# Residual kept by token tiles: norms on rows, 512-column out and down products, gates as broadcast rows

## The chip, the cores and the metric

The kernel runs on one core of one Trainium2 chip. The core has five engines that run side by side and meet by semaphores: TensorE (PE; its weight loads are listed apart as PEld), VectorE (DVE), ScalarE (ACT), GpSimd (POOL) and SyncE (SP, here used for loads). The metric is the device time of one execution in microseconds; lower is better. All data is fp32.

## The reference, cut to what matters

A two-layer backbone runs over 640 tokens of width 1024: 128 context tokens and 512 latent tokens, each group with its own modulation vectors. One layer:

```
shift1, scale1, gate1, shift2, scale2, gate2 = split(silu(cond) @ w_mod + b_mod)      # 6 x 1024
h = rmsnorm(x, g_mix) * (1 + scale1) + shift1
z = h @ w_in                                  # 2720 columns, feed four token mixers
branches = four mixer outputs (256 each) @ w_branch                                   # to 1024
mixed = sum(sigmoid(h @ w_gate + b_gate) * branches) @ w_out
x = x + gate1 * mixed
h2 = rmsnorm(x, g_ffn) * (1 + scale2) + shift2
u = h2 @ w_up + b_up; conv = depthwise width 3 over tokens; a, gg = split(conv)       # 2 x 2816
x = x + gate2 * ((silu(gg) * a) @ w_down)
```

A last rmsnorm with g_final gives the outputs. The mixers (retention, window attention, differential attention, latent attention) are the same before and after the change.

## The kernel before, in words

Every large product is made of three products of rounded parts: each fp32 operand is split in a high part (fp32r) and a low part (the rest), and high x high, low x high and high x low are summed in PSUM. For weights ACT rounds the high part (`round_unit`, L1436) and POOL subtracts the low part (L767); for activations ACT and DVE do it. Weights come in units of up to 1 MB in the order of `weight_units`, through three raw buffers and two pairs of high/low slots. Every engine runs one list of instructions in the order in which the program issues them; nothing is reordered between them, and all order is written out by hand.

The residual x is held channel by channel: 8 tiles k of 128 channels on the partitions, 640 tokens along the free dimension. What hangs on that:

- The in product (`in_product`, L914) holds 128 tokens of h as the stationary operand and moves 512 columns of the weights. Its output z has tokens on partitions.
- The gate, out, up and down products (`product3`, L819) hold 128x128 of the weights and move tokens, 320 or 322 at a time (two halves), in the out product's tiles 5 to 7 and the first two up tiles 256 and 384.
- The out product's result is added to x by `add_to_x` (L2230), one operation per token piece, with the gate as a per-partition scalar. `take_out` follows with the squares (`add_square`, L2222 and L2224). The sum over channels needs PE: `part_sums` (L880) multiplies the squares by ones, ACT takes the root, DVE the reciprocal and a diagonal, and `spread_part` (L887) brings it back to all partitions. `part_norm` then scales, modulates and splits x into h_hi and h_lo, in two parts of 256 and 384 tokens, so that the first up tiles (`first_up`) can start on the first part.
- The down product (`down_tiles`, `down_part`) runs in three groups of 8, 8 and 6 activation tiles. In the last group the last k of the first tiles is put off until its activation is ready. `take_down` adds the result to x.
- At a layer's start `mod_pair` (L841) computes the first eight modulation columns in four pairs: per pair 16 matmuls of 256 columns, each on a quarter of the array, the four k of a quarter round summed afterwards by `fold_pair` (L850). In both layers they lie in or ahead of the first in product.
- At the start of the kernel 40 transposes (L791) bring x into this layout, at the end 40 transposes (L1404) bring it back; `token_sums`, `spread_rstd` and L1397 do the sums in between.
- x itself is stored in DRAM while the mixers use its room as the sum `acc`, and is loaded back on ACT's queue during the last gates.

The prediction's steps touch `in_product`, the out loop, `first_up`, `down_tiles`, `mod_pair` on PE, the norm functions on ACT and DVE, and SP's list of loads.

Of the kernel before, what the change touches and what calls it, by code (L numbers as in the profile page):

```python
# [60 lines left out]
ACT_SLOTS = 12  # L61
# [3 lines left out]
def mlp_order():  # L65

    items = []
    for g, (j0, nj) in enumerate(UP_GROUPS):
        first = j0 + (AHEAD if g else 0)
        items += [("up", j) for j in range(first, j0 + nj)]  # L70
        if g + 1 < len(UP_GROUPS):
            n0 = UP_GROUPS[g + 1][0]
            items += [("up", j) for j in range(n0, n0 + AHEAD)]
        items += [("down", (g, mp)) for mp in range(4)]
    return items
# [52 lines left out]
def weight_units():  # L128

    mod = iter(MOD_ORDER)  # L130
    win = lambda g: [("in", (g, half), True) for half in range(2)]
    mods = lambda n: [("mod", next(mod), False) for _ in range(n)]
    gate = lambda n, mp: [("gate", (n, mp), True)]
    first, second = win(0)
    units = mods(2) + [first] + mods(4) + [second] + mods(2) + win(1) + gate(0, 0) + gate(0, 1) + win(2)
    units += gate(0, 2) + mods(1) + gate(0, 3) + mods(3) + [("in", (3, 0), True)] + mods(2) + [("in", (3, 1), True)] + win(4) + win(5)
    units += gate(1, 0) + gate(1, 1) + mods(2) + gate(1, 2) + mods(1) + gate(1, 3) + mods(1) + gate(2, 0)
    units += [("uq", 0, False)] + gate(2, 1) + [("ukv", 0, False)] + mods(2) + gate(2, 2) + mods(1) + gate(2, 3)
# [6 lines left out]
OUT_TILES = [(m, None) for m in range(5)] + [(m, 0) for m in range(5, KD)] + [(m, 1) for m in range(5, KD)]  # L145
OUT_BANK = {(5, 0): 4, (6, 0): 5, (7, 0): 2, (5, 1): 3, (6, 1): 1, (7, 1): 5}
OUT_BEHIND = {(7, 0): (3, None), (5, 1): (3, None), (6, 1): (4, None), (7, 1): (6, 0)}
CUT = 2 * P
PARTS = (slice(0, CUT), slice(CUT, TOK))
PART_TILES = (range(0, 2), range(2, T))  # L150
WHOLE = ((0, 0, CTX), (1, CTX, TOK))
PIECES = (((0, 0, CTX), (1, CTX, CUT)), ((1, CUT, TOK),))


UNITS = weight_units()
N_UNITS = len(UNITS)
N_SPLIT = sum(split for _, _, split in UNITS)
RAW = 3
WS = 2
SPLIT_KEYS = [(kind, i) for kind, i, split in UNITS if split]  # L160
LOW_BY_VECTOR = [("in", (0, 0)), ("in", (0, 1))]
LOW_BY_POOL = [key for key in SPLIT_KEYS if key not in LOW_BY_VECTOR]
# [18 lines left out]
def part_slot(li, s):  # L181

    return WS if SLOT[s] == WS else (SLOT[s] + li * FLIP) % WS

# [94 lines left out]
def build(nc, a, outs):  # L279
# [3 lines left out]
    with ctx:  # L283
# [12 lines left out]
        x = at("x", [P, KD, TOK])  # L296
# [6 lines left out]
        vcol = at("vcol", [P, 317])  # L303
        cond = at("cond", [P, 16])
# [76 lines left out]
        acc = x  # L381
        x_saved = nc.dram_tensor("x_saved", [P, KD, TOK], F32).ap()

        sq = at("sq", [P, TOK], offset=BASE + 82272)
        ss = at("ss", [P, TOK], offset=BASE + 84832)
        t1 = at("t1", [P, 2, TOK], offset=NT + 5120)
        sq_b = at("sq_b", [P, 3, TOK - CUT], offset=NT + 10240)
        diag = at("diag", [P, T, P], offset=NT + 15360)

        a_hi = at("a_hi", [P, ACT_SLOTS, PADDED], F32R, offset=BASE)  # L390
        a_lo = at("a_lo", [P, ACT_SLOTS, PADDED], F32R, offset=BASE + 30816)
        FB = BASE + 61632
# [5 lines left out]
        x_tm = at("x_tm", [P, T, D], offset=BASE)  # L398
        y_tm = at("y_tm", [P, T, D], offset=BASE + 20480)
        g_fin = at("g_fin", [P, D], offset=BASE + 40960)  # L400
# [19 lines left out]
        def x_ready(m, part):  # L420

            return OUT_TILES.index((m, part)) + 1

# [3 lines left out]
        def pair_col(li, p):  # L427

            return 5 * BANK if p else 3 * BANK if li else 7 * BANK + P
# [16 lines left out]

        raw_loaded = [Signal(f"raw_loaded{i}", loaded_count(max(range(i, N_UNITS, RAW)))) for i in range(RAW)]
        hi_done, lo_done = Signal("w_high_ready", N_SPLIT), Signal("w_low_ready", len(LOW_BY_POOL))
# [1907 lines left out]
```

## Time and profile before

| | us |
|---|---|
| median of 3 runs | 2431.77 |
| lowest, highest | 2429.27, 2432.41 |
| profiled execution | 2432.2 |
| its span, first to last instruction | 2430.4 |

The page says that PE is busy for 2363.8 us, PEld for 2144.0, DVE for 1244.4, ACT for 879.1 and POOL for 731.8. The mean granted clock of PE is 0.993 of full speed. A matmul's busy time includes its way through the array, so consecutive matmuls overlap in the records: what a stream of them costs is read from the distance of their starts, not from their mean duration. An fp32 matmul that is not rounded leaves two records, a transpose one. "Idle before <- X" names what the engine waited for.

### The profile page before, as it was taken

How to read it: one execution, taken by the hardware profiler on the slowest of the kernel's cores; microseconds unless marked ns; L12 is line 12 of the kernel's file. 1: busy time of each engine (PE TensorE's matmuls, PEld its weight loads, DVE VectorE, ACT ScalarE, POOL GpSimd, SP SyncE). 2: the span in 40 equal slices, each digit the busy share in tenths (PEclk: the TensorE clock that was granted, in tenths of full speed). 3: DMA queues.
4: the chain of work that ended last, by engine and by line, in shares of the span. 5: the costliest groups of instructions: out<-in, count | busy, mean ns of one | idle time of the engine just before them, and what ended most of it. 6: DMA issues, size and time to landing. Idle time of an engine off the chain costs nothing.

```text
span 2430.4 us, 38405 instructions
## 1 busy us (share of the span) xinstructions
PE 2363.8 (97%) x16085; PEld 2144.0 (88%) x16085; DVE 1244.4 (51%) x2251; ACT 879.1 (36%) x1642; POOL 731.8 (30%) x500
## 2 busy tenths in 40 slices
PE   7999999999999999999999999999999999999998
PEld 5887787788999999999978878887889999999997
DVE  5426247534347762753763362673433677447356
ACT  4335245534324431332243352555343243223231
POOL 0321221101342453444312203210113435435432
PEclk9999999999999999999999999999999999999999
DMA  8413221222331322222271132312232312222211
GB/s 291 143 55 122 66 91 59 74 70 87 109 92 53 104 70 70 87 70 61 79 269 55 53 124 72 102 46 71 87 104 85 98 53 70 87 70 70 87 53 53
DMA packets 234154, 216.48 MB, mean 89 GB/s; under 512 B 8310, under 2 KB 217598, under 8 KB 233726
## 3 DMA queue, kind: packets, MB, share of 16 engines
q1 hardware_dynamic: 225911, 193.77, 25.0%
q10 hardware_dynamic: 8071, 20.25, 2.4%
q8 instruction: 128, 2.10, 0.3%
q14 instruction: 44, 0.36, 0.0%
HBM read 204.92 MB, written 9.08 MB: 88 GB/s over the span
## 4 chain that ended last, share of the span: by engine, by line
PE 88%; DVE 5%; ACT 3%; POOL 2%; issue 1%; DMA 0%; ACTq 0%; DVEq 0%
PE ps L819 58%; PE ps L914 11%; PE ps L968 4%; PE ps L1021 2%; POOL w_lo L767 2%; PE ps L1038 2%; PE ps L1000 2%; PE ps L1010 2%; PE ps L829 1%; ACT w_hi L1436 1%; DVE h_lo L1891 1%; PE ps L989 1%; DVE t L1883 1%; PE ps L859 1%; PE ps L1214 1%
## 5 line engine op out<-in xcount | busy, mean ns | idle before, releaser
L767 POOL TENSOR_TENSOR w_lo<-raw,w_hi 128x512 fp32r<-128x512 f32 x488 | 718.9, 1503 | 1664.3 <-ACT w_hi L1436 1048.8
L819 PE MATMUL ps<-h_hi,w_hi 128*128 128x320 f32 (+2 forms) x2368 | 618.4, 314 | 4.0 <-POOL w_lo L767 4.0
L819 PE MATMUL ps<-h_lo,w_hi 128*128 128x320 f32 (+2 forms) x2368 | 608.8, 310 | 0.0
L819 PE MATMUL ps<-h_hi,w_lo 128*128 128x320 f32 (+2 forms) x2368 | 608.7, 310 | 0.0
L819 PEld LDWEIGHTS ps<-h_hi,w_hi 128*128 128x128 f32 x2368 | 415.1, 189 | 8.8 <-issue 4.3
L819 PEld LDWEIGHTS ps<-h_lo,w_hi 128*128 128x128 f32 x2368 | 415.0, 189 | 0.8
L819 PEld LDWEIGHTS ps<-h_hi,w_lo 128*128 128x128 f32 x2368 | 415.0, 188 | 0.0
L1436 ACT ACTIVATE w_hi<-raw 128x2048 fp32r<-128x2048 f32 (+2 forms) x110 | 203.7, 1851 | 307.3 <-PE ps L819 219.0
L1986 DVE TENSOR_REDUCE stat<-ps 128x1 f32<-128x640 f32 (+3 forms) x160 | 107.9, 674 | 174.7 <-PE ps L1010 113.9
L914 PE MATMUL ps<-w_hi,h_hi 128*128 128x512 f32 (+1 forms) x480 | 182.8, 381 | 6.8 <-DVE h_lo L1891 3.8
L914 PE MATMUL ps<-w_hi,h_lo 128*128 128x512 f32 (+1 forms) x480 | 180.1, 375 | 0.0
L914 PE MATMUL ps<-w_lo,h_hi 128*128 128x512 f32 (+1 forms) x480 | 180.1, 375 | 0.0
L2230 DVE SCALAR_TENSOR_TENSOR x<-ps,mod,x 128x128 f32<-128x128 f32 (+4 forms) x192 | 72.9, 434 | 192.7 <-PE ps L819 192.0
L819 PE MATMUL ps<-a_hi,w_hi 128*128 128x322 f32 x704 | 162.6, 312 | 2.2 <-DVE a_lo L2297 1.4
L2282 DVE TENSOR_SCALAR conv<-u_pad,vcol 128x642 f32<-128x642 f32 x88 | 91.9, 1044 | 141.4 <-ACT u_pad L1788 139.8
L819 PE MATMUL ps<-a_hi,w_lo 128*128 128x322 f32 x704 | 161.7, 311 | 0.0
L819 PE MATMUL ps<-a_lo,w_hi 128*128 128x322 f32 x704 | 161.4, 310 | 0.0
L1796 ACT ACTIVATE usig<-conv 128x642 f32<-128x642 f32 x44 | 32.7, 744 | 261.3 <-DVE conv L2286 261.3
L968 PE MATMUL ps<-o_t,w_br 128*128 128x320 f32 x384 | 125.3, 450 | 0.0
L819 PEld LDWEIGHTS ps<-a_hi,w_hi 128*128 128x128 f32 x704 | 118.9, 190 | 3.3 <-DVE a_lo L2297 1.9
L2284 DVE SCALAR_TENSOR_TENSOR conv<-u_pad,vcol,conv 128x642 f32<-128x642 f32 x88 | 118.4, 1345 | 3.1
L819 PEld LDWEIGHTS ps<-a_lo,w_hi 128*128 128x128 f32 x704 | 118.8, 189 | 0.0
(299 smaller groups left out, 3330.0 us busy)
## 6 DMA issues: line engine op xcount, KB each, us to landing
raw<-in_w_mod SPq DMA_DIRECT2D x48, 1024.0 KB, 5.1
raw<-in_w_up SPq DMA_DIRECT2D x88, 512.0 KB, 4.6
raw<-in_w_gate SPq DMA_DIRECT2D x32, 1024.0 KB, 5.7
raw<-in_w_in SPq DMA_DIRECT2D x20, 1024.0 KB, 5.5
raw<-in_w_down SPq DMA_DIRECT2D x16, 1024.0 KB, 5.2
w_br<-in_w_branch ACTq DMA_DIRECT2D x8, 1024.0 KB, 5.0
raw<-in_w_out SPq DMA_DIRECT2D x8, 1024.0 KB, 5.2
raw<-in_w_down SPq DMA_DIRECT2D x8, 768.0 KB, 4.8
```

Source lines behind the costliest of these rows:

```text
L767: ins = nc.gpsimd.tensor_tensor(w_lo[part_slot(li, s)][:, c0:c1], raw[u % RAW][:, c0:c1], w_hi[part_slot(li, s)][:, c0:c1].bitcast(F32), A ...
L819: ins = mm(out, w_at(w_hl[wi]), at_(x_hl[xi]), start=first and q == 0, stop=final and q == 2)
L914: last = mm(bank(b, 0, n), (h_hi, h_lo)[xi][:, k, t * P:(t + 1) * P], w_hl[wi][:, k4, :], start=k == 0 and q == 0, stop=k == KD - 1 and q ...
L968: last = mm(bank(FILL_BANK[("branch", q)], 0, HALF), w_br[:, k, m * P:(m + 1) * P], o_t[n % 2][:, k, half * HALF:(half + 1) * HALF], start ...
L1000: last = mm(bank(2 * m2, col, col + n), query(br, t, h, m2), keys(br, h, m2, k0, n), start=True, stop=True)
L1010: last = mm(bank(2 * (m % 2), col, col + n), query(br, t, h, 0), keys(br, h, 0, k0, n), start=True, stop=True)
L1021: last = mm(ps[64 * odd:64 * odd + 64, 6 * BANK + 64 * h:6 * BANK + 64 * h + P], values(br, b, h + odd), turned(a_ + odd)[:, j, :], start= ...
L1436: act_(w_hi[part_slot(li, s)][:, 0:n], raw[u % RAW][:, 0:n], ACT.Copy).then_inc(hi_done.sem, 1)
L1986: V.tensor_reduce(stat[:, 0, col], bank(b, 0, nk), AX.X, ALU.max).then_inc(vstep.sem, 1)
L2230: ins = stt(x[:, k, c0:c0 + n], src, mod[:, gate0 + k, w:w + 1], x[:, k, c0:c0 + n], ALU.mult, ALU.add)
L2282: ts(cv, u[:, 0:PADDED], col(WCONV[0]), col(BCONV), ALU.mult, ALU.add).then_inc(vstep.sem, 1)
L2284: stt(cv, u[:, 1:1 + PADDED], col(WCONV[1]), cv, ALU.mult, ALU.add).then_inc(vstep.sem, 1)
```

## The change

It turns the residual to 5 tiles t of 128 tokens on the partitions, with 1024 channels along the free dimension, and everything that reads or writes it with it.

- The out and down products hold 128 tokens of activations and move 512 weight columns, like the in product (halves dh of the output, halves kh of the contraction). The weight units of both are cut accordingly. The last half of each (dh = 1) runs in the order of `SWEEPS`: tiles 0 to 2 are finished ahead of 3 and 4.
- The gate is now a row: SP stores mod's gate columns to DRAM and ACT loads them back broadcast over the partitions. The add becomes two operations, `add_rows`: product by gate row, then the sum.
- The norm runs by token tile: ACT squares with an accumulated sum, root; DVE reciprocal; ACT scales; PE turns the tile by 8 transposes; DVE modulates 8 pieces of 128; ACT rounds; DVE subtracts. The sums by PE, the diagonal and its spreading go. Layer 0's first norm works channel by channel (`turn_channels`) on x scaled beforehand.
- The four modulation pairs of layer 1 move into layer 0's MLP, behind down sweeps. Each pair now has 64 matmuls of 64 columns that sum over k in PSUM, and DVE turns 32x32 blocks instead of the folding on PE.
- The transposes of x at the start and of y at the end go; ten activation slots instead of twelve.

The core of the diff:

```diff
-    units += [("out", mp, True) for mp in range(4)]
-    units += [(kind, i, True) for kind, i in MLP]
+    units += [("out", (dh, kh), True, li) for dh in range(2) for kh in range(2)]
+    for kind, i in MLP:
+        units.append((kind, i, True, li))
+        if kind == "down" and i in PAIR_AT and li + 1 < DEPTH:
+            units += [("mod", m, False, li + 1) for m in MOD_ORDER[2 * PAIR_AT[i]:2 * PAIR_AT[i] + 2]]
+PAIR_AT = {(0, 0, 0): 0, (0, 0, 1): 1, (1, 0, 0): 2, (1, 0, 1): 3}
+ROW_BANK = ((0, 1, 2, 3, 4), (0, 1, 5, 6, 7))
+TURN_BANK = {"in": ((2, 3), (1, 4), (3, 5), (6, 7), (4, 5)), "ffn": ((2, 3), (0, 1), (4, 5), (2, 3), (6, 7))}
+SWEEPS = ((0, (0, 1, 2)), (1, (0, 1, 2)), (0, (3, 4)), (1, (3, 4)))
...
+                def mod_pair(layer, p):   # PE
...
                     for second, i in enumerate((p, p + 4)):
-                        w = raw_unit("mod", i)
+                        w = raw_unit("mod", i, layer)
                         for k in range(KD):
-                            q0 = 32 * (k % 4)
-                            last = mm(ps[q0:q0 + 32, c0:c0 + 256], cond_c[:, k, 2 - 2 * second:34 - 2 * second], w[:, k, :],
-                                      start=second == 0 and k < 4, stop=second == 1 and k >= 4)
+                            turns = w[:, k, :].rearrange("p (b g j) -> p g b j", g=4, j=32)
+                            for g in range(4):
+                                last = mm(ps[32 * g:32 * g + 32, c0 + 64 * second:c0 + 64 * second + 64].rearrange("p (b j) -> p b j", j=32),
+                                          cond_c[:, k, 2:34], turns[:, g], start=k == 0, stop=k == KD - 1)
...
+                def turn_rows(layer, which, t):   # PE
+                    pe.wait_ge(xn_done.sem, ROW_BASE[layer, which] + t + 1)
+                    if t >= 2:
+                        pe.wait_ge(t1_done.sem, TURN_BASE[layer, which] + t - 1)
+                    if which == "in" and t == 3:
+                        pe.wait_ge(x_down.sem, counts(layer - 1)(x_down, n_down))
+                    if which == "ffn" and t == 4:
+                        pe.wait_ge(x_out.sem, counts(layer)(x_out, 2 * T))
+                    for k in range(KD):
+                        last = tr(bank(TURN_BANK[which][t][k // 4], k % 4 * P, k % 4 * P + P), xn[:, t % 2, k * P:(k + 1) * P], ident)
...
+                def out_sweep(dh, kh, tiles):   # PE; down_sweep is alike, with nj // 2 k a half
...
+                            for q, (xi, wi) in enumerate(((0, 0), (0, 1), (1, 0))):
+                                last = mm(bank(b), (mix_hi, mix_lo)[xi][:, k, row_cols(t)], w_hl[wi][:, k4, :],
+                                          start=k == 0 and q == 0, stop=k == KD - 1 and q == 2)
...
+                        if dh == 1 and (kh, t) in ((0, 3), (0, 4), (1, 3)):
+                            turn_rows(li, "ffn", {(0, 3): 0, (0, 4): 1, (1, 3): 2}[kh, t])
...
+                        if (j, tokens, k) == (0, 0, 3):   # in first_up
+                            turn_rows(li, "ffn", 3)
+                        if (j, tokens, k) == (1, 0, 0):
+                            turn_rows(li, "ffn", 4)
...
+                    first_product({(0, 0): lambda: turn_rows(li, "in", 3), (0, 1): lambda: turn_rows(li, "in", 4)})
...
+                def norm_rows(which):   # ACT
+                    rms = lambda t: row_rms(which, t, xn[:, t % 2, :])
+                    rms(0)
+                    rms(1)
+                    row_scaled(which, 0)
+                    row_scaled(which, 1)
+                    rms(2)
+                    row_scaled(which, 2)
+                    round_unit()
+                    row_high(which, 0)
+                    row_high(which, 1)
+                    rms(3)
+                    row_scaled(which, 3)
+                    row_high(which, 2)
+                    if which == "in":
+                        round_unit()
+                    rms(4)
+                    row_scaled(which, 4)
+                    row_high(which, 3)
+                    row_high(which, 4)
...
+                def norm_rows(layer, which, add, between):   # DVE
+                    add(0)
+                    add(1)
+                    rstd(0)
+                    rstd(1)
+                    add(2)
+                    rstd(2)
+                    row_modulated(layer, which, 0)
+                    row_modulated(layer, which, 1)
+                    between()
+                    row_low(layer, which, 0)
+                    row_low(layer, which, 1)
+                    add(3)
+                    row_modulated(layer, which, 2)
+                    rstd(3)
+                    row_low(layer, which, 2)
+                    add(4)
+                    rstd(4)
+                    row_modulated(layer, which, 3)
+                    row_low(layer, which, 3)
+                    row_modulated(layer, which, 4)
+                    row_low(layer, which, 4)
...
+                def add_rows(t, dh, parts, gated, done, n):   # DVE
+                    tt(parts[:, n % 2, :], bank(ROW_BANK[dh][t]), grow[:, min(t, 1), cols], ALU.mult).then_inc(gated.sem, 1)
+                    ve.wait_ge(gated.sem, now(gated, n))
+                    tt(x[:, t, cols], x[:, t, cols], parts[:, n % 2, :], ALU.add).then_inc(done.sem, 1)
```

In layer 1's norm `between` is DVE's half of the low part of the first in unit. `t1_done` counts modulated tiles, `xn_done` scaled ones, `x_down` and `x_out` added ones.

## Rows read from the trace of the kernel before

**Rows 1.** The page: busy time by engine
```profile
PE 2363.8 (97%) x16085; PEld 2144.0 (88%) x16085; DVE 1244.4 (51%) x2251; ACT 879.1 (36%) x1642; POOL 731.8 (30%) x500
```

**Rows 2.** Stretches: us, busy of PE, PEld, DVE, ACT, POOL (x), granted clock, DMA share, GB/s
```profile
791.00:1173.00 382.00, 382.00 (x2595) 382.00 (x2596) 211.57 (x222) 117.58 (x181) 170.29 (x107) 1.00 0.26 78
1173.00:1217.00 44.00, 42.87 (x287) 42.35 (x286) 34.19 (x45) 9.70 (x12) 14.26 (x9) 1.00 0.21 72
```

**Rows 3.** Timeline of PE, layer 0's MLP: start us, us, what
```profile
889.53 0.45 PE L819 MATMUL ps<-a_hi,w_hi 128*128 128x322 f32 x2
...
946.82 0.45 PE L819 MATMUL ps<-h_hi,w_hi 128*128 128x320 f32 x2
...
1172.65 0.46 PE L819 MATMUL ps<-a_hi,w_hi 128*128 128x322 f32 x2
...
1217.09 0.60 PE L780 MATMUL ps<-const,rows 96*128 96x96 f32 x4
```

**Rows 4.** Timeline of PE, layer 0's out product to the third up tile
```profile
686.02 0.56 PE L819 MATMUL ps<-mix_hi,w_hi 128*128 128x320 f32 x2 [0.98 <-DVE gprod L2213]
...
743.30 0.28 PE L819 MATMUL ps<-h_hi,w_hi_up 128*128 128x256 f32 x1
...
775.87 0.31 PE L819 MATMUL ps<-h_hi,w_hi 128*128 128x320 f32 x1
```

**Rows 5.** Chain of waits, in order of time: start us, us, what
```profile
66.31 27.49 PE ps L914 x120
...
1261.30 27.49 PE ps L914 x120
```

**Rows 6.** DVE by form: out<-in xcount | busy, mean ns | idle before
```profile
L1883 DVE SCALAR_TENSOR_TENSOR t<-x,scl,ps 128x128 f32<-128x128 f32 x48 | 15.0, 345 | 6.8 <-PE ps L887 3.6 <-PE ps L873 2.6
L2138 DVE TENSOR_TENSOR st_dec<-ps,dmask 128x512 f32<-128x512 f32 x10 | 6.9, 692 | 30.6 <-PE ps L1101 30.6
```

**Rows 7.** Timeline of DVE and POOL, layer 0's last down tiles
```profile
1186.01 0.83 DVE L2297 TENSOR_TENSOR a_lo<-act,a_hi 128x642 fp32r<-128x642 f32 x1 [0.81 <-ACT a_hi L1801]
1192.59 1.80 DVE L2224 TENSOR_TENSOR ss<-ss,sq 128x640 f32<-128x640 f32 x1
...
1190.59 4.95 POOL L767 TENSOR_TENSOR w_lo<-raw,w_hi 128x512 fp32r<-128x512 f32 x3 [9.57 <-ACT w_hi L1436]
1256.22 5.02 POOL L767 TENSOR_TENSOR w_lo<-raw,w_hi 128x512 fp32r<-128x512 f32 x4 [54.72 <-ACT w_hi L1436]
```

**Rows 8.** Timeline of ACT: a square at the start, a table load, a root, a rounding
```profile
13.26 1.06 ACT L1417 ACTIVATE y_tm<-x_tm 128x1024 f32<-128x1024 f32 x1 [5.89 <-DMA x_tm<-in_x_sample]
...
1220.02 1.28 ACT L1479 ACT_TABLE_LOAD   x1
1221.58 0.27 ACT L1479 ACTIVATE st<-ps,eps_c 128x5 f32<-128x5 f32 x1 [0.27 <-PE ps L866]
...
734.79 1.92 ACT L1436 ACTIVATE w_hi<-raw 128x2048 fp32r<-128x2048 f32 x1 [1.47 <-PE ps L819]
```

**Rows 9.** Timeline of PE: short matmuls, and a product behind them
```profile
34.38 1.93 PE L841 MATMUL ps<-raw,cond_c 128*32 128x256 f32 x32
...
104.06 1.15 PE L1089 MATMUL ps<-z,kd 128*64 128x64 f32 x32
...
157.39 2.29 PE L932 MATMUL ps<-const,ret_sq 128*128 128x2 f32 x20
161.08 0.63 PE L914 MATMUL ps<-w_lo,h_hi 128*128 128x512 f32 x1
...
179.53 0.71 PE L1147 MATMUL ps<-const,z 128*128 128x128 f32 x5
```

**Rows 10.** Timeline of PE, first product of layer 0
```profile
28.30 0.77 PE L914 MATMUL ps<-w_hi,h_hi 128*128 128x512 f32 x1 [3.63 <-DVE h_lo L1891]
```

**Rows 11.** Timeline of the end: the last squares' sums on PE, the last outputs on DVE
```profile
2415.20 1.42 PE L1397 MATMUL ps<-ones,ss 128*128 128x1 f32 x10 [3.11 <-DVE ss L2224]
...
2422.02 5.08 DVE L2333 SCALAR_TENSOR_TENSOR y_tm<-ps,st,g_fin 128x1024 f32<-128x1024 f32 x4 [0.35 <-PE ps L1404]
```

More of the change, by code:

```diff
@@ L125, with weight_units @@
 MOD_ORDER = [i for p in range(4) for i in (p, p + 4)] + list(range(8, 24))
[L128 to L133, printed above, removed]
+PAIR_AT = {(0, 0, 0): 0, (0, 0, 1): 1, (1, 0, 0): 2, (1, 0, 1): 3}
+def weight_units(li):
+    mod = iter(MOD_ORDER[8 if li else 0:])
+    win = lambda g: [("in", (g, half), True, li) for half in range(2)]
+    mods = lambda n: [("mod", next(mod), False, li) for _ in range(n)]
+    gate = lambda n, mp: [("gate", (n, mp), True, li)]
@@ L151 @@
 WHOLE = ((0, 0, CTX), (1, CTX, TOK))
[L152 to L157, printed above, removed]
+LAYER_UNITS = [weight_units(li) for li in range(DEPTH)]
+UNITS = [unit for layer in LAYER_UNITS for unit in layer]
+UNIT_AT = {(li, kind, i): u for u, (kind, i, _, li) in enumerate(UNITS)}
 RAW = 3
 WS = 2
-SPLIT_KEYS = [(kind, i) for kind, i, split in UNITS if split]
+SPLIT_KEYS = [(kind, i) for kind, i, split, _ in LAYER_UNITS[0] if split]
@@ L161 @@
+assert SPLIT_KEYS == [(kind, i) for kind, i, split, _ in LAYER_UNITS[1] if split]
+N_SPLIT = len(SPLIT_KEYS)
 LOW_BY_VECTOR = [("in", (0, 0)), ("in", (0, 1))]
-LOW_BY_POOL = [key for key in SPLIT_KEYS if key not in LOW_BY_VECTOR]
 def part_slots():
@@ L1309, in up_tile @@
+                out_sweep(0, 0, range(T))
+                out_sweep(0, 1, range(T))
+                for kh, tiles in SWEEPS:
+                    out_sweep(1, kh, tiles)
                 def up_tile(j):
@@ new lines, in turn_mod_vectors, with down_tiles @@
+                def turn_mod_vectors():
+                    pe.wait_ge(rows_in.sem, counts(li + 1)(rows_in, 16 * N_ROWS))
+                    tr(bank(7, 0, 64), rows[0:64, 0, :], ident[0:64, 0:64]).then_inc(mvec_t.sem, 1)
+                def down_tiles(g, dh, kh):
+                    if (g, dh) == (len(UP_GROUPS) - 1, 1):
+                        for kh_, tiles in SWEEPS if kh else ():
+                            down_sweep(g, dh, kh_, tiles)
+                        return
+                    down_sweep(g, dh, kh, range(T))
+                    if (g, dh, kh) in PAIR_AT and li + 1 < DEPTH:
+                        pe.wait_ge(up_done.sem, now(up_done, min(FFT, sum(UP_GROUPS[g]) + AHEAD)))
+                        if (g, dh, kh) == (0, 0, 0):
+                            turn_mod_vectors()
+                        mod_pair(li + 1, PAIR_AT[g, dh, kh])
@@ L1803, in _ @@
                 sc.wait_ge(cache_out.sem, now(cache_out, 16 * 10))
-            sc.wait_ge(yss_mm.sem, 1)
-            act_(st5[:, 3, 0:T], bank(4, 0, T), ACT.Sqrt, bias=eps_c[:], scale=1.0 / D).then_inc(yst_done.sem, 1)
+            for t in range(T):
+                row_rms("end", t, y_tm[:, t, :])
             sc.wait_ge(cache_out.sem, DEPTH * cache_out.per)
@@ new lines, in row_modulated @@
+                def row_modulated(layer, which, t):
+                    ve.wait_ge(turn_mm.sem, TURN_BASE[layer, which] + t + 1)
+                    i, w = (0, 1)[which == "ffn"], min(t, 1)
+                    for k in range(KD):
+                        src = bank(TURN_BANK[which][t][k // 4], k % 4 * P, k % 4 * P + P)
+                        ins = ts(hn[:, t % 2, k * P:(k + 1) * P], src, scl[:, i, k, w:w + 1], mod[:, 24 * i + k, w:w + 1], ALU.mult, ALU.add)
+                    ins.then_inc(t1_done.sem, 1)
```

754 lines of the change are left out of this document (345 added, 409 removed).

## The prediction

> **What bounds the kernel now.** I read the page first: TensorE (PE) is busy for 97% of the span [rows 1]. The stretches then say where that share is whole: in the MLP, from 791 to 1173 us, PE has no idle time at all, while VectorE (DVE) is busy for 55% and GpSimd (POOL) for 45% of it [rows 2]. So any matmul time saved there shortens the kernel one for one, and any work added to PE lengthens it. Last I read the places where the order changes: out product to up product, down product to the next layer's in product, the start and the end. There a chain over PE, ScalarE (ACT) and DVE decides, and there the change puts another chain.
>
> The profiled execution took 2432.2 us, its span 2430.4; the median of the three runs is 2431.8. I sum against the profiled one.
>
> **(a) Fewer, wider matmuls: -12.8 us.** Before, group 0 of the down product is 8 m x 8 k x 3 x 2 = 384 matmuls of 321 columns on average in 946.82 - 889.53 = 57.3 us, 0.149 us each [rows 3]. A product with 512 moving columns is in the trace already: 120 in 27.49 us, 0.229 us each [rows 5]. The columns stay the same; 0.465 ns a column becomes 0.447. Per layer 1056 matmuls become 660: 157.6 against 151.2 us, so -6.4, twice -12.8. The out product (384 matmuls become 240, 55.0 us) is counted in (c).
>
> **(b) End of the down product: +4.0.** The last activation is ready at 1186.84, 14.2 us after the last up tile's matmuls end at 1172.65 [rows 3, 7]. Before, other matmuls covered all but 1.1 us of it [rows 2]. Now the sweep of the first three k is 45 x 0.229 = 10.3 us, and two k of the next tile add 1.4: 2.5 us are left open, and some 0.6 for the last weight unit, whose rounding waits for the whole sweep ahead (1.5 ACT, 5.0 POOL, against 6.2 of cover). That is 2.0 more per layer.
>
> **(c) Out product to up product: +9.7.** Before it took 775.87 - 686.02 = 89.9 us [rows 4]. After: 240 x 0.229 = 55.0; the first two up tiles, 61,440 columns at 0.465 = 28.6; the row norm puts 5 x 8 transposes on PE, at (0.71 - 0.27)/4 = 0.11 us each [rows 9] 4.4; the wait at the start of the product falls by 1.0 (it needs seven gates read, not eight) [rows 4]. That is 87.0 before any gap.
>
> The gaps. Per token tile DVE has two gated adds (0.69 for 512 elements from PSUM, 0.66 for the one in SBUF), eight modulations of 128 columns (0.345 each, overlapping to about 0.28: 2.2 together), one low part of 1024 (0.83 for 642 elements, so 1.2 to 1.3) [rows 6, 7]. ACT has a square and a root (1.06 + 0.27, and 0.2 for the hand-over, my estimate), a scaling and a rounding (1.05 each) [rows 8]. The order is fixed on both. I count from the end of the last out sweep. Low parts of tiles 0 and 1 end at -2.2 and -1.0. Only behind them does DVE add tile 3, whose matmuls ended at -3.6: 0.5. Its square on ACT and DVE's modulation of tile 2 (to 2.8) run side by side; the reciprocal is queued behind that modulation; scaled 4.1. PE wants it at 2.9: gap 1.3. Tile 4's add is queued behind low part 2, which waits for ACT: 8.0; scaled 11.1; PE wants it at 8.7: gap 2.5. Then modulation, rounding and low part of tiles 3 and 4 in turn: 19.4; PE is through with tiles 0 and 1 at 17.1: gap 2.4. Together 6.2.
>
> POOL makes low weights in that time. A DVE operation with two SBUF inputs that falls beside one takes about 1 us longer: 1.80 us for 640 elements beside POOL, 0.83 alone for 642 [rows 7]. If all low parts and adds up to tile 3 meet one, the gaps are 9.2. I take the middle, 7.7: 94.7 against 89.9, +4.8 per layer. The Trainium skill (SBUF — State Buffer, Who interferes with whom) has it that the shared port pair is an exclusive lock, so that the loser waits for a whole instruction. By that rule a PSUM-sourced modulation waits for nobody, and the gaps are 9.2, not 12 or more; the trace agrees with the 1 us per meeting, not with a stall of every operation.
>
> **(d) Layer boundary: +19.5.** Before: 1217.09 to the second in group at 1261.30, 44.2 us [rows 3, 5]. After, by the same walk with sweeps of 2.06 and 2.75 us: ten sweeps 27.5, turns of tiles 3 and 4 1.8, turns of tiles 0 to 2 with a small wait 2.9, a table load of 1.28 for the root, now ahead of the chain [rows 8], 1.3. The first low part is late by 1.3, since rounding the weights (1.92) and DVE's share of their low part stand ahead of it. The large gap: the turn of tile 3 waits until all five tiles are added, because it takes over the bank of tile 4; that add is queued on DVE behind low part 2, behind ACT's rounding, behind the scaling of tile 3. PE wants the turn at 4.0 and gets it at 11.5: 7.5 us. Lock 1.0. The next group's first weights come 1.9 late (slot freed only 5.5 us before; 1.9 ACT, 5.0 POOL [rows 7, 8]). Before the first product of layer 0 PE idled 3.6 us [rows 10], and its first matmuls of 512 columns started 0.43 instead of 0.23 us apart, each record 0.63 long as in the slow stretch of [rows 9]; I take 3.0 for such a stretch at 1.2 GHz. Sum 48.2, +4.0.
>
> Here belong the four pairs of modulation products of layer 1. Before, they lie inside the 44.2 at 1.87 us a pair (32 records [rows 9]). After, they lie in the MLP, where PE is full, and each pair is 2 x 8 x 4 = 64 matmuls of 64 columns, 128 records. The trace has no such form. From below: the columns alone, four column groups at once, as before: 1.9 us. From above: the pitch of a 256-column record, (1.93 - 0.39 for the last one)/31 = 50 ns: 6.4. The nearest row is the 64-column matmul of the retention states, 32 records in 1.15 us, 30 ns each [rows 9]: 3.8 a pair, which I take. 4 x 3.84 and one transpose = 15.5. Sum of (d): +19.5.
>
> The Trainium skill (TensorE: Matmul & The Clock Gate, Wait — 56ns, not 53.3ns?) says that with decoding in the sequencer each matmul costs some 62 ns however short it is. By that rule a pair is 7.9 us; the 30 ns rows speak against it.
>
> **(e) Start: +12.9.** x no longer passes PE, but the first product now waits for: five squares and roots in turn on ACT from 13.26 with one table load, to 21.2 [rows 8]; the last scaling on DVE, 23.6; turn of channel 0, 24.4; only then the first pair on PE (3.8), 28.3; its take-up, modulation, rounding and, behind half a microsecond of low weights and the modulation of channel 1, the low part: 33.1 against 28.3 before [rows 10], +4.8. Then within the product: three pairs, +1.97 each (5.9), three foldings less (-1.1), six turns of five transposes (+3.3).
>
> **(f) End: -10.2.** Before, from the last matmul (3.1 us ahead of 2415.20) at 2412.1 to 2430.4: 18.3 us, with sums, root, 40 transposes and five outputs in turn [rows 11]. After, only tile 4 is behind the last matmul: add 1.4, square and root 1.6, reciprocal 0.2, output 1.3, hand-overs 0.3, and the last store 3.3 (2430.4 less the end of DVE at 2427.1 [rows 11]): 8.1.
>
> Nothing for the rest: the stores of the gate rows and their broadcast loads stand behind weight loads with 40 us of slack (if that cover fails, a load is late by a few us); the DVE adds in the MLP rise from 9 to 14 us a group on an engine with 45% idle; ten activation slots instead of twelve are never waited for. The pairs' weights hold two of three raw buffers, which leaves about 2 us of cover at the second half of a down group.
>
> Sum: -12.8 + 4.0 + 9.7 + 19.5 + 12.9 - 10.2 = +23.1, so 2432.2 + 23.1 = 2455.3; 0.4 less against the median: 2455.
>
> **Rivals.** *Cheap pairs.* The short matmuls run four wide and cost 1.9 a pair: 2455 - 8 x 1.97 = 2439. For it: the long ones do run four wide; against: the only short row has 30 ns. *Hidden rows (the other side).* The row chain keeps up with PE: DVE and ACT interleave better than I walk, and no turn is waited for. It decides from the point where tile 3 is scaled before PE's first sweep behind the down product ends. Then 2 x 7.7, 7.5, 1.3, 1.0 and 3.0 go, 28.2: 2427, faster. Against it: the add of tile 4 is queued behind low part 2 in the program itself. *Half clock.* A run of short matmuls lowers the clock: behind 20 records of 2 columns (2.3 us), products of 512 columns took 0.43 us a piece for some 3.4 us (0.63 a record [rows 9]). Behind each of eight pairs that is +1.7: 2469. *Issue bound.* At the 50 ns end, 8 x 2.6 more: 2476. *Not as described.* If the wide matmul did not keep its 0.229 us with activations stationary, (a) falls away; the in product is of just this form, so hardly.
>
> **How the numbers follow.** My forecast 0.45, cheap pairs 0.22, hidden rows 0.15, half clock 0.12, issue bound 0.06. A measurement here can tell about 0.2% (5 us) from no change. Low end: cheap pairs without the lock and the slow stretch, 2439 - 7 = 2432; high end: half clock, with the upper gaps of (c) and (d), 2474. Faster: hidden rows and a little of cheap pairs, 0.17; within 0.2% 0.05; slower 0.78.
>
> **What would show it.** After: L819's 512-column down matmuls at 0.229 us; 128 records of the pair product in 3.8 us; PE gaps before the transposes of tiles 3 and 4, released by ACT's scaling, 1 to 3 us in each out product and some 7 at the boundary; the first product at 33 us; 8 us behind the last matmul. A boundary gap under 2 us, or pairs under 2.5 us, would make the prediction wrong.

## The result, and the profile after

The changed kernel takes 2487.9 us (median of 4 runs, 2479.1 to 2492.6), the kernel before 2430.5: ratio 1.023 [1.020, 1.026], slower by 2.3%. Forecast were 2455 us and a range of 2432 to 2474: the sign was right, the size was 33 us short, outside the range. The profiled execution took 2487.5 us, its span 2485.7, against 2430.4 before. What follows is the difference of the spans, 55.3 us. One execution of e3 (3724 us, at a granted clock of 0.585) is in no median or ratio of this text.

The page, part 1 (busy time, share of the span):

```profile
PE 2363.1 (95%) x15742; PEld 2067.4 (83%) x15742; DVE 1236.2 (50%) x2169; ACT 902.2 (36%) x1644; POOL 735.5 (30%) x506
```

PE's share fell from 97% [rows 1] to 95%: it works little more than before, and waits more. Whom it waits for (view of waits of PE: us in total, times, longest):

```profile
PE ps L831 <- DVE w_lo L2276: 15.6, 2, 9.3
PE ps L938 <- POOL w_lo L788: 11.0, 2, 9.1
PE ps L876 <- DVE xn L1891: 9.5, 1, 9.5
PE ps L889 <- DVE x L2295: 7.9, 1, 7.9
PE ps L831 <- DVE h_lo L1947: 6.6, 4, 2.6
...
PE ps L1386 <- POOL w_lo L788: 5.6, 2, 2.8
PE ps L889 <- ACT xn L1497: 5.5, 5, 2.3
...
PE ps L1386 <- DVE a_lo L2334: 4.4, 2, 2.2
```

Rows four, five and seven are the waits of the row norm, near my walk. The first, the second and the sixth, 32 us together, wait for weights. My prediction gave these 1.9 us, at the boundary, and else nothing.

Stage by stage, in us; each mark is the start of a PE row in the timelines, as [rows 3, 4, 5]. An in group is the 120 matmuls of one 512-column unit of `w_in`, a late gate tile one of those left until behind the mixers, and a down group one of the three groups of activation tiles:

```
stage                                    before  after   diff  forecast
start to second in group, layer 0          66.3   78.1  +11.8   +12.9
to the first late gate tile               548.1  550.1   +2.0     0
gate and branch tiles, to out product      71.6   81.5   +9.9    -1.0
out product to first down group           203.5  209.6   +6.1    +5.8
first down group (two pairs)               57.3   64.5   +7.3    +5.5
to the last down group (two pairs)        225.8  231.8   +6.0    +5.4
last down group, boundary, to 2nd group    88.7   98.2   +9.6    +4.3
to the first late gate tile, layer 1      548.0  550.0   +2.0     0
gate and branch tiles                      71.6   78.3   +6.7    -1.0
out product to first down group           203.5  209.6   +6.1    +5.8
first to last down group (no pairs)       283.1  280.4   -2.7    -4.7
last down group to the end                 62.9   53.6   -9.4    -9.9
sum                                                     +55.4   +23.1
```

Of the 32 us that I missed, 18.6 are in two stages that the change seemed only to shorten, the gate and branch tiles. The chain of waits in the first of them (start us, us, what):

```profile
628.54 18.93 DMA w_br<-in_w_branch
647.47 0.02 issue
647.49 1.92 ACT w_hi L1795
649.41 0.02 issue
649.43 2.30 DVE w_lo L2276
651.74 0.14 issue
651.87 58.02 PE ps L831 x384
```

The load of branch 3's weights takes 18.9 us. In the kernel before the same load, issued at 614.72, landed in 4.8 us, and PE did not wait for it (view of the tile `w_br` in the window of that issue alone):

```profile
DMA to landing us min/median/max: 4.8/4.8/4.8
```

In layer 1 it is 15.9 us in place of 5.2. Around its issue SP issues the four stores of the gate rows (timeline of SP; then from the view of DMA issues, KB each, median us to landing):

```profile
625.62 5.73 SPq L757 DMA_DIRECT2D gate_rows<-mod  x4
637.25 62.63 SPq L768 DMA_DIRECT2D raw<-in_w_out  x4
```

```profile
gate_rows<-mod SPq DMA_DIRECT2D x8, 4.0 KB, 15.8
```

Four KB take 15.8 us, three times as long as a weight unit of 1024 KB (4.8 to 5.4 us in the page's medians). Each store is 1024 pieces of 4 bytes.

The chain behind the first pair in the MLP, and at the boundary:

```profile
933.58 1.97 PE ps L855 x128
...
935.98 10.88 DMA raw<-in_w_down
...
946.88 1.92 ACT w_hi L1455
...
948.87 5.42 POOL w_lo L788 x4
...
954.34 29.70 PE ps L1386 x120
...
1276.08 1.94 PE ps L889 x8
...
1304.33 0.44 PE ps L801 x4
...
1304.86 0.50 DVE vcol L1873
...
1306.34 0.23 DVE dsum L2116
...
1306.59 0.02 ACT dec_t L1632
...
1306.90 1.81 ACT w_hi L1455
...
1308.77 4.95 POOL w_lo L788 x4
...
1313.86 29.12 PE ps L938 x120
```

A pair is 128 records in 1.97 us, half of what I took. But the down unit behind it is loaded late: it is issued at 935.98, when the pair has ended, and takes 10.9 us. At the boundary the weights are not late by their slot: ACT's rounding stands behind an exponential, which waits for DVE's `dsum`, which waits for `vcol`, which PE turns (L801) behind the first product.

A wait costs more than its length. Granted clock and busy time in stretches (page's columns) during and behind the wait ahead of the branch tile:

```profile
642.60:651.80 9.20, 0.00 (x0) 0.00 (x0) 2.29 (x1) 4.31 (x3) 0.00 (x0) 0.63 0.51 91
651.90:661.90 10.00, 10.00 (x58) 10.00 (x59) 4.70 (x6) 1.48 (x2) 5.00 (x4) 0.83 0.37 123
661.90:680.00 18.10, 18.10 (x126) 18.10 (x125) 6.88 (x7) 4.87 (x5) 4.32 (x3) 1.00 0.10 30
```

Behind 9.3 us without a matmul the clock is at 1.2 instead of 2.4 GHz for the first third of 10 us: 1.7 us more. It does not come behind every wait. Of the two waits of 2.8 us ahead of a down unit the first has it behind it, the second has not (same columns):

```profile
954.30:964.30 10.00, 9.96 (x36) 8.00 (x37) 0.00 (x0) 1.91 (x1) 5.03 (x4) 0.83 0.80 248
1131.40:1141.40 10.00, 10.00 (x43) 8.14 (x44) 0.00 (x0) 1.92 (x1) 5.03 (x4) 1.00 0.79 245
```

Over the span the granted clock is 0.983, before 0.993.

### The profile page after: what moved, and what is told of

Same layout as the page of the kernel before. It is cut to its first block, busy times and chain, and to the rows that moved or that the text cites. A ratio compares the mean times of both kernels' runs of the same rounds, so it can differ in the third digit from the quotient of the medians.

```text
span 2485.7 us, 37639 instructions
## 1 busy us (share of the span) xinstructions
PE 2363.1 (95%) x15742; PEld 2067.4 (83%) x15742; DVE 1236.2 (50%) x2169; ACT 902.2 (36%) x1644; POOL 735.5 (30%) x506
## 4 chain that ended last, share of the span: by engine, by line
PE 86%; DVE 6%; ACT 3%; DMA 3%; POOL 1%; issue 1%; SPq 0%; ACTq 0%; DVEq 0%
PE ps L831 42%; PE ps L938 11%; PE ps L1386 10%; PE ps L992 4%; PE ps L1314 4%; PE ps L1045 2%; PE ps L1062 2%; PE ps L1024 2%; PE ps L1034 2%; POOL w_lo L788 1%; DMA w_br<-in_w_branch 1%; DVE hn L1941 1%; PE ps L842 1%; PE ps L905 1%; DMA raw<-in_w_down 1%
## 5 line engine op out<-in xcount | busy, mean ns | idle before, releaser
L1386 PE MATMUL ps<-w_hi,a_hi 128*128 128x512 f32 x440 | 175.5, 399 | 10.0 <-POOL w_lo L788 5.6
L938 PE MATMUL ps<-w_hi,h_hi 128*128 128x512 f32 (+1 forms) x440 | 167.9, 382 | 17.4 <-POOL w_lo L788 11.0
L1386 PE MATMUL ps<-w_lo,a_hi 128*128 128x512 f32 x440 | 174.8, 397 | 0.0
L1386 PE MATMUL ps<-w_hi,a_lo 128*128 128x512 f32 x440 | 174.7, 397 | 0.0
L2319 DVE TENSOR_SCALAR conv<-u_pad,vcol 128x642 f32<-128x642 f32 x88 | 90.1, 1024 | 156.3 <-ACT u_pad L1830 154.7
L938 PE MATMUL ps<-w_lo,h_hi 128*128 128x512 f32 (+1 forms) x440 | 166.1, 377 | 0.0
L938 PE MATMUL ps<-w_hi,h_lo 128*128 128x512 f32 (+1 forms) x440 | 165.4, 376 | 0.0
L1830 ACT ACTIVATE u_pad<-ps,vcol 128x128 f32<-128x128 f32 (+3 forms) x264 | 91.6, 447 | 91.7 <-PE ps L831 91.7
L2323 DVE SCALAR_TENSOR_TENSOR conv<-u_pad,vcol,conv 128x642 f32<-128x642 f32 x88 | 116.7, 1326 | 3.1
L2321 DVE SCALAR_TENSOR_TENSOR conv<-u_pad,vcol,conv 128x642 f32<-128x642 f32 x88 | 116.6, 1325 | 3.1
L1600 ACT ACTIVATE probs<-ps,stat 128x640 f32<-128x640 f32 (+3 forms) x136 | 90.2, 664 | 67.7 <-DVE stat L2063 67.1
```

Of the source, the lines that this page charges most:

```text
L938: last = mm(bank(b, 0, n), (h_hi, h_lo)[xi][:, k, t * P:(t + 1) * P], w_hl[wi][:, k4, :], start=k == 0 and q == 0, stop=k == KD - 1 and q ...
L1386: last = mm(bank(b), (a_hi, a_lo)[xi][:, sl, at_], w_hl[wi][:, k4, :], start=k == 0 and q == 0, stop=k == nj - 1 and q == 2)
L1600: act_(prob(m)[:, 0:nk], bank(score_bank(m), 0, nk), ACT.Exp, bias=bias, scale=SCALES[br], accum_out=stat[:, 2, m % 8:m % 8 + 1]).then_inc ...
L1830: ins = act_(u[:, d0:d0 + n], bank(b, c0, c0 + n), ACT.Identity, bias=bias)
L2321: stt(cv, u[:, 1:1 + PADDED], col(WCONV[1]), cv, ALU.mult, ALU.add).then_inc(vstep.sem, 1)
L2323: ins = stt(cv, u[:, 2:2 + PADDED], col(WCONV[2]), cv, ALU.mult, ALU.add)
```

## Experiments

Times are medians; ratios are to the kernel before, run on the same chip. The changed kernel has 1.023.

**The gate rows' stores (e1, e4, e2).** e1 stores in pieces of 32 bytes:

```diff
-  ... gate_rows[li, v, c_].rearrange("(k p) -> p k", p=P), mod[:, 16 + 24 * v:24 + 24 * v, c_] ...
+  ... gate_rows[li, v, c_].rearrange("(p k) -> p k", k=KD), mod[:].rearrange("p n w -> p (n w)")[:, 32 + 48 * v + 8 * c_:40 + 48 * v + 8 * c_] ...
```

> The changed kernel with the gate rows stored in pieces of 32 bytes (eight neighbouring values of a partition) instead of 4 bytes; this leaves the gate rows in the wrong order, so the gates are wrong in value, all else is the same work. Theory P (small packets): the four stores of 1024 pieces of 4 bytes fill the DMA queues just when branch 3's weights are loaded; that load took 18.9 us instead of 7.7. With 512 pieces in all it lands in about 8 us, PE's wait of 9.3 us (layer 0) and 6.3 us (layer 1) ahead of branch_tile(0) goes, and with it the slow clock behind it: -16 to -18, about 2471 us. Rival Q (the load is late for another reason: it shares the queues with three weight loads): the wait stays, 2487 us.

Measured 2463.6, ratio 1.013 [1.011, 1.015]: -24. The wait is gone: gate and branch tiles take 70.5 us in either layer in place of 81.5 and 78.3, which is 18.9 (the two waits, 15.6, and the slow clock behind them). The stores land in 4.0 us, branch 3's load in 5.0 and 6.1; the 7.7 us that the expectations give for it before is the start of its rounding, which stands behind other work of ACT. The other 5 us of the median are in no stage with a changed order (the stage from the second in group to the first late gate tile, the mixers' stage, took 547 instead of 550 in layer 0). In e4 the kernel before gets only the stores:

> The kernel before, with only the four 4-byte stores of the gate vectors of the change added at the same place of SP's order (nobody reads them). Theory P: branch 3's load (7.7 us before) takes about 19 us, PE waits 8 to 10 us in layer 0 and 5 to 7 us in layer 1 ahead of the third branch's first tile: +15 to +18, about 2447 us. Rival Q: the stores alone cost nothing, 2431 us.

Measured 2446.7, ratio 1.0064 [1.0049, 1.0079]: +15 from 16 KB a layer that nobody reads. `w_br` lands in up to 17.3 us and PE waits 11.4 us for its low part, 7.7 the longest. The two stages grow by 10.1 and 6.4 us. Theory P is shown from both sides. Size and number of the pieces changed together in e1 (4096 of 4 bytes, 512 of 32), so which of the two decides is not shown. The Trainium skill (DMA: Bandwidth & Descriptors, Specifications) puts the piece from which a transfer runs at line rate at 512 bytes. Pieces of 4 and of 32 bytes are both below it, and took 15.8 and 4.0 us here. e2 moves the stores to ACT's queue behind `mix_high(1)`:

> The changed kernel, right in its values, with the same 4-byte stores issued by ACT behind the branch's take-up and two mix tiles, some 25 us later. Theory P: branch 3's load lands in about 8 us, both waits go, and the stores now fall beside the loads of the out weights and of x, which have slack: 2471 us, as with wide pieces. Rival Q: 2487. Rival R (the stores only hand their delay on to the next load): one of the waits appears again ahead of the out product, 5 to 10 us a layer, 2480 to 2487 us.

Measured 2478.0, 1.019 [1.017, 1.021]. The old wait is gone, a new one is there: 3.7 us at most and 7.1 in both layers for `gprod`. The two stages take 75.7 and 75.9 us, 5 us each over e1. Timeline of ACT:

```profile
646.80 2.28 ACTq L1796 DMA_DIRECT2D gate_rows<-mod  x4
649.12 11.92 ACTq L1776 DMA_DIRECT2D x<-x_saved  x1
661.14 0.79 ACT L1765 ACTIVATE sig<-ps,vcol 128x640 f32<-128x640 f32 x1 [13.61 <-issue]
```

The issue of the next load stands for 11.9 us, and with it ACT. Rival R was right that the delay is handed on; it went to the issuing engine, not to a load.

**The rounding on ACT (e3).**

```diff
                 load_branch(0)
+                if li: round_unit()
                 sc.wait_ge(tab_arg.sem, now(tab_arg, 1))
                 (two exponentials)
-                round_unit()
+                if not li: round_unit()
```

> The changed kernel with one move on ACT in layer 1: the rounding of the second in group's first weights ahead of the exponents of the retention decay. Theory S (queued behind): the rounding stood behind an exponent that waits for DVE, which waits for the turned vectors, which PE turns only behind the first product; so the weights came 9.1 us late. Moved ahead, the rounding starts when the slot is released by the first half of tile 4 (about 1293), low part ready by 1300, before PE asks at 1304.8: -9.1, and the slow clock of the second group (29.1 us instead of 27.5) goes too: -10 to -11, about 2477 us. Rival T (the slot or the load is the late one): the wait shrinks by 2 us at most, 2485 us.

Measured 2478.4 (three runs), 1.019 [1.017, 1.022]: -9.5. The second group starts 1.8 us after the first product ends, not 9.5, and takes its old time (chain):

```profile
1303.42 27.47 PE ps L938 x120
```

That is 7.7 + 1.7 = 9.4 us less, as theory S said.

**Order of the weight loads (e5).** The units of pairs 1 and 3 are loaded behind down unit (g, 1, 0):

```diff
-        if kind == "down" and i in PAIR_AT and li + 1 < DEPTH:
+        at = {(g, dh, kh) if not kh else (g, 1, 0): p ...}; if kind == "down" and i in at ...
```

> The changed kernel with the two weight units of the second pair of each down group (pairs 1 and 3) loaded behind the down unit that follows them instead of ahead of it; all products keep their order. Theory U (ring): the third down unit's load was issued 14 us too late because it stood in SP's order behind two pair units whose buffers PE frees only with pair 0; it landed 10.9 us after, beside them, and PE waited 2.8 us twice, with a slow-clock stretch of some 1.6 us behind each wait. Moved ahead of them, it lands some 5 to 6 us earlier: both waits go, -6 to -9, about 2480 us. Rival V (rounding slot, not the load): the waits stay, 2487.

Measured 2480.5, 1.021 [1.019, 1.022]. Both waits of 2.8 us are gone; the two down groups take 60.1 and 60.0 instead of 64.5 and 62.8 us: -7.2, theory U. Of that 5.6 is the waits, the rest the slow clock, which is not the same in every execution: in e1, e2, e3, e6 and e7, where these groups have their old order, the two take 124.7 to 127.3 us together (127.3 in the changed kernel), so the move is worth 4.6 to 7.2.

**DVE's order in the row norm (e6).**

```diff
-  add(3); row_modulated(2); rstd(3); row_low(2); add(4); rstd(4)
+  add(3); add(4); rstd(3); row_modulated(2); row_low(2); rstd(4)
```

> The changed kernel with DVE's order in the row norm changed: tile 4's gated add directly behind tile 3's, and tile 3's reciprocal ahead of tile 2's modulation. My walk of the boundary had the turn of tile 3 wait because tile 4's add stood behind low part 2: it waited 7.9 us. Theory W: the turn is wanted at 1268.2 and comes at about 1270 instead of 1276: -5 to -6 at the boundary with a little slow clock; in each out product the waits of 2.3 and 2.6 us shrink to some 1 us together: -2 a layer; in all -8 to -10, about 2478 us. Rival X (ACT is the bound: its squares, scalings and roundings stand in a fixed order): the gap moves to tile 2's low part, 2 us gained, 2485.

Measured 2475.5, 1.018 [1.017, 1.020], but the trace does not bear theory W out. PE's turns of tiles 3 and 4 at the boundary:

```profile
1265.56 1.09 PE L889 MATMUL ps<-const,xn 128*128 128x128 f32 x8 [2.26 <-ACT xn L1497]
...
1272.56 1.75 PE L889 MATMUL ps<-const,xn 128*128 128x128 f32 x7 [3.17 <-ACT xn L1497]
```

7.9 us of waiting became 5.4, now for ACT, and the stage from the last down group to the second in group is as long as before the edit (98.4 against 98.2): rival X. In the profiled execution, 7.6 us shorter than that of the changed kernel, 6.4 are in the mixers' stage of layer 0, which took 544 instead of 550 us and whose order is the same. The times of the changed kernel's versions spread wider (this one 2472 to 2480, the kernel before 2429 to 2432), and half-clock stretches fall differently in them; why, and how much of the -12 is the edit's, is not shown.

**Together (e8, e9, e10).** e8 has all moves so far with e7's; e9 lets SP issue the stores ahead of out unit (1, 0) and has no e7; e10 adds:

```diff
-  turn_channels(0); mod_pair(0, 0)
+  mod_pair(0, 0); turn_channels(0)
```

> All five moves that keep the values right, together: stores later, rounding ahead, ring order, adds, alignment. If their causes are apart they add: 17 + 10 + 7 + 9 + 2.6 = 46, about 2442 us, still 0.5% above the kernel before; if they share a cover the sum is smaller, 2450 to 2460.

> As the kernel with all moves together, but the 4-byte stores issued by SP ahead of the third out weight unit (some 45 us later than in the changed kernel) instead of by ACT, and without the change of place of mix_hi. Theory P': in the kernel that let ACT issue them, ACT's next issue (the load of x) stood 11.9 us, so the gates of the mix tiles came late and PE waited 5.2 and 4.7 us for the gated product. [...] Issued by SP, whose weight loads have 40 us of slack there, both waits go: -9.9 and a little slow clock, about 2447 us. Rival R' (the packets then delay the out weights or the gate rows' broadcast): a wait ahead of the third out unit or ahead of the first gated add, 2452 to 2458 us.

> The kernel before this one in the list, and on PE the first modulation pair ahead of the turn of channel 0 at the start. Theory: x has to pass squares, roots and scaling until 22.6 us, while the pair's weights are there earlier; the pair (3.6 us at half clock) is then done by 20, and only turn, modulation, rounding and low part are left behind 22.6: the first in product starts at about 28.5 to 29 us instead of 32.4: -3.5 us. Rival: the pair's weights land only at about 22 us, and nothing is gained.

Measured 2458.3 (1.012), 2446.4 (1.0066 [1.0049, 1.0083]) and 2439.2 (1.0033 [1.0022, 1.0045]). Taken one at a time the five moves of e8 changed the median by -9.9, -9.5, -7.4, -12.4 and +2.3, -36.9 in all; together they give -29.6, not the -46 that I expected. e8 has the `gprod` wait of e2 (9.9 us). In e9 it is gone and no new wait took its place. In e10 the first in product starts at 28.2 instead of 32.4 us.

**Distance from start to start in 512-column products (e7, e11 to e14).** I took 0.229 us a matmul from the in product [rows 5], whose 27.49 us hold the whole last record; from start to start it is 0.227, in out and down products 0.232 to 0.233. e7 leaves out an unused tile, so that `BASE`, where `mix_hi` and `a_hi` start, comes to a multiple of 64 bytes (128 above one of 256):

```diff
-        token = at("token", [P, 1])
```

> The changed kernel with an unused 4-byte tile left out, so that the buffers behind it, mix_hi and mix_lo among them, start at a multiple of 64 bytes instead of 32 above one. Theory Y (place of the stationary operand): 512-column products whose stationary operand starts at such a multiple (the in product) follow each other every 0.227 us, the out product every 0.233. Then the out product comes down to 0.227: 480 matmuls by 5.5 ns, -2.6 us. The down product keeps 0.232, since its rows are 642 elements long and start at other multiples. Rival Z (it is the traffic of other engines beside it, or the order of accumulation): both stay at 0.232 to 0.233, no change of time.

Measured 2490.2, 1.0245 [1.0230, 1.0260]; the out product stays at 233.3 ns: theory Y falls for 64 bytes. e11 gives half of the products another stationary operand:

> The changed kernel with the first half of each out product (dh 0) and the first group of each down product reading the normed rows (h_hi, h_lo) as stationary operand instead of the mixed rows and the activations; this makes x wrong, the work is the same. Open: why 512-column products follow each other every 0.227 us in the in product and every 0.232 to 0.233 in the out and down products, 1800 of them. Theory H (it hangs on the stationary buffer): the two changed stages come to 0.227, the others stay; -5 ns by 960 = -5 us. Rival I (it hangs on the stage, what runs beside it or the weights' slots): all stay at 0.232 to 0.233.

```diff
-  ... (mix_hi, mix_lo)[xi][:, k, row_cols(t)] ...
+  ... ((mix_hi, mix_lo) if dh else (h_hi, h_lo))[xi][:, k, row_cols(t)] ...
```

In the changed stages 226.7 to 227.5 ns, in the others 231.5 to 233.4: theory H. e12 reads 16 sweeps (60 matmuls each) from moved places of four buffers, `flat[:, o:o + P]` with another offset each:

> The changed kernel with the stationary operand of 16 sweeps of the down product (two groups of each layer, 60 matmuls of 512 columns each) read from 12 places: the normed rows at their own place and moved by 4, 8, 32, 64, 128, 256 and 512 bytes, the activations at a multiple of 1024 bytes, at 32 above a multiple of 64, and pairs of one buffer low and one high in SBUF; this makes x wrong, the work is the same. The normed rows lie at bytes 22016 to 62976 of a partition, the activations and the mixed rows from 139168 on, the moving weights between. Theory A (alignment): the pitch is 0.227 us wherever the start is a multiple of 64 (or 128, 256, 512) bytes, in either region, and 0.232 to 0.233 elsewhere; the moved rows tell which multiple. Theory B (region): all sweeps with low buffers take 0.227, whatever the shift, and all with high buffers 0.232 to 0.233, aligned or not; mixed pairs in proportion to the loads from each. In both the other stages stay and the time is within 5 us of 2487.

```
h_hi, h_lo in place           227.2    moved by 32 / 64 / 128 bytes   233.4 / 233.4 / 232.5
moved by 256 / 512 bytes      227.2 / 227.1    moved by 4 / 8 bytes   232.5 / 230.7
a_hi and a_lo, multiples of 1024    227.3    a_hi at BASE, a_lo       231.1
h_hi and a_lo, a_hi and h_lo  226.9, 226.7    h_lo and a_lo           226.7
h_hi alone / a_hi alone       227.1 / 226.7    a_lo and a_lo + 64     231.0
```

(ns a matmul, from starts in the timeline; `a_hi` is at a multiple of 1024 where nothing else is said.) The operands' names tell which sweep is which. The first matmuls of layer 1's first four sweeps, which are `h_hi, h_lo` moved by 8 bytes, `a_hi` and `a_lo` at multiples of 1024, `a_hi` at `BASE` with `a_lo`, and `h_hi` with `a_lo`:

```profile
2139.68 0.40 PE L1405 MATMUL ps<-w_hi,h_hi 128*128 128x512 f32 x1
...
2153.53 0.40 PE L1405 MATMUL ps<-w_hi,a_hi 128*128 128x512 f32 x1
...
2167.17 0.39 PE L1405 MATMUL ps<-w_hi,a_hi 128*128 128x512 f32 x1
...
2181.05 0.39 PE L1405 MATMUL ps<-w_hi,h_hi 128*128 128x512 f32 x1
```

That is 13.85, 13.64 and 13.88 us for 60 matmuls: slow, fast, slow. Region is out: high buffers alone, low ones alone and one of each are all fast. A multiple of 256 bytes fits all 16 sweeps: 226.7 to 227.3 ns where every block starts at one, 230.7 to 233.4 where one of the two buffers, or both, does not. The exceptions that the expectation of e13 names come from counting the sweeps of layer 1 one place off (its 227.3 for a move by 8 bytes is the sweep behind it). e13 packs tiny tiles so that `BASE` is a multiple of 256, e14 keeps the activations without their two pad columns (`a_hi`, `a_lo` as `[P, ACT_SLOTS, TOK]`, written in two pieces), so that every block starts at one:

> The corrected kernel with the pair first, and five tiny tiles packed into one (and one unused left out) so that the mixed rows (mix_hi, mix_lo) and the first activation slot start at a multiple of 256 bytes; all values are right. In the run with moved operands the normed rows took 227.1 ns a matmul at their place, 233.3 and 233.4 moved by 32 and 64 bytes, 232.5 by 128, 227.3 by 256 and 226.6 by 512; a move by 8 bytes (227.3) and two sweeps with high buffers do not fit. Theory A' (a multiple of 256 bytes): the out product comes from 233.4 to about 227 ns: 480 matmuls by 6.4 ns, -3 us, about 2436 us; the down product, whose rows start elsewhere, stays near 232. Rival B' (the place against that of the moving weights decides, not the multiple): the out product stays at 233 or takes another value.

> The kernel before this one in the list (mixed rows at a multiple of 256 bytes), and the activation slots kept without their two pad columns, so that every 128-row block of a_hi and a_lo starts at a multiple of 256 bytes too; ACT and DVE write a slot in two pieces (128 and 512 columns) instead of one of 642. All values are right. Theory A' (the multiple of 256 bytes): the down product comes from 231 to 233 ns a matmul to 227: 1320 matmuls by 4.5 to 5 ns = -6 to -6.6 us; the second piece costs ACT and DVE some 0.2 us a tile, hidden but for the last tile of each layer (+0.4 in all): about 2425 us, 0.2 to 0.3% under the kernel before. Rival B' (the place against the moving weights): the down product stays at 231 to 233, 2431 us, even with the kernel before.

Chain of waits of the changed kernel, then of e14 (whole down groups of layer 1):

```profile
2151.91 55.73 PE ps L1386 x240
...
2320.28 55.69 PE ps L1386 x240
```

```profile
2091.84 54.43 PE ps L1384 x240
...
2258.90 54.42 PE ps L1384 x240
```

Out product 227 ns in e13 (down 231 to 234), down product 227 ns in e14, as theory A' said. Why a start at a multiple of 256 bytes is faster is open. e13 takes 2431.3 us (10 runs, 1.0003 [0.9994, 1.0013]), e14 2430.9 (11 runs, 2422 to 2437; 0.9997 [0.9986, 1.0007]). The 6 us that 1320 down matmuls should save from e13 to e14 (231.8 against 227.1 ns) don't show in the median: the spread is larger. So the best version is even with the kernel before, 57 us under the changed one, and doesn't beat it.

## Why the prediction was wrong

The step that failed is "nothing for the rest: the stores of the gate rows and their broadcast loads stand behind weight loads with 40 us of slack". I looked at SP's own order and at bytes. The stores lie beside a load of another queue, branch 3's, whose cover is small: it landed 14.1 us later than before and PE waited 9.3, so some 4.8. And what they cost does not go by their 16 KB a layer but by how these are cut, 4096 pieces of 4 bytes. They cost 18.9 us in the two stages (e1, e4); against the forecast these stages make 18.6 of the 32 us missed. The rest is in the steps below.

- **(a) -12.8: sized too high.** 1320 down matmuls at 0.232 instead of 0.229 give back 4 us, 480 out matmuls at 0.2333 another 2. Where the stationary operand starts was the cause (e11 to e14).
- **(b) +4.0: about half.** The last activation is waited for 2.2 us, as forecast (2.5); no weight unit is late.
- **(c) +9.7: right** (the stage grew by 6.1 a layer, forecast 5.8). The gaps are 0.7 + 2.3 + 0.2 + 2.6 = 5.8 for forecast 7.7; the out product's 0.2333 us a matmul and half-clock stretches behind the gaps make up for it.
- **(d) rows +4.0: the wait of tile 3's turn was right** (7.9 for 7.5). The next weights were 9.1 us late and not 1.9: I counted slot, rounding and low part, but not what stands ahead of the rounding on ACT. The vectors' turn moved behind the first product, and everything chained to it moved along: 7.7 us of waiting and 1.7 of slow clock (e3).
- **(d) pairs +15.5: half.** 15 ns a record, not 30: rival *cheap pairs* was right on the price, and by itself takes 7.5 off here. The 62 ns a matmul that the Trainium skill (TensorE: Matmul & The Clock Gate, Wait — 56ns, not 53.3ns?) gives for decoding in the sequencer do not bind here: a matmul of 64 columns, two records, took 31. But I wrote that the pairs' weights leave "about 2 us of cover" and booked no cost: it was 2.8 us short, twice, 7.2 us with the clock (e5).
- **(e) +12.9: right** (+11.8). The first product began at 32.4 for forecast 33.1:

```profile
22.55 1.30 PE L876 MATMUL ps<-const,xn 128*128 128x128 f32 x5 [9.55 <-DVE xn L1891]
23.78 3.58 PE L855 MATMUL ps<-raw,cond_c 128*32 128x64 f32 x128
29.60 0.74 PE L876 MATMUL ps<-const,xn 128*128 128x128 f32 x5 [2.24 <-DVE t L1927]
32.39 0.77 PE L938 MATMUL ps<-w_hi,h_hi 128*128 128x512 f32 x1 [2.05 <-DVE h_lo L1933]
```

- **(f) -10.2: right.** From the last matmul's end (2478.1) to the end 7.6 us, forecast 8.1, before 18.3.
- **Half clock.** I priced it behind pairs, where it did not come (1.97 us a pair inside the MLP). It came behind waits: 1.5 to 1.7 us behind those of 9.3, 6.3 and 9.1 us, 1.6 behind the 1.9 us ahead of layer 0's second in group, and behind one of the two of 2.8 us.

*Hidden rows* is refuted: PE waits for rows at every place where I said so (0.7 to 2.6 us in the out product, 7.9 at the boundary).

## What to carry to other kernels

Ask of every new transfer in how many pieces and of what size it is cut, which loads of every queue are in flight beside it, and which engine issues next behind it. When an instruction moves past others, follow what hangs on it through the other engines' orders: a rounding that nobody touched came 9 us late since a transpose had moved. And count with a half-clock stretch behind a wait on TensorE: here 1.5 to 1.7 us behind the long ones, and behind one of two waits of 2.8 us.

## What the hardware showed that I had not expected

- Four stores of 4 KB each in pieces of 4 bytes took 11 to 21 us to land and stretched a 1 MB load beside them from 4.8 and 5.2 to 18.9 and 15.9 us; in pieces of 32 bytes they took 4.0 us, and the load 5.0 and 6.1.
- Behind such stores the next issue on the same engine stood 11.9 us, and the engine with it (e2).
- 64 matmuls of 64 columns in four column groups, 128 records, took 1.97 us, 31 ns each.
- A 512-column matmul follows the one before after about 227 or 231 to 233 ns by where its stationary operand starts: 227 at every multiple of 256 bytes tried (e11 to e14), 230.7 to 233.4 when moved off one by 4, 8, 32, 64 or 128 bytes.
